# Hybrid decoder trunk: the output of layers 1, 3 and 4 is turned by VectorE and transfers inside SBUF, not by TensorE

## What is computed

```python
for i in range(DEPTH):
    hn = rmsnorm(x, norm_g[i])
    kind, j = i % N_MIXERS, i // N_MIXERS
    if kind == 0:
        y = diff_attention(hn, da_w_in[j], da_w_out[j], ...)
    elif kind == 1:
        y = sliding_window_attention(hn, sw_w_in[j], sw_w_out[j], ...)
    else:
        y = mlstm(hn, ml_w_in[j], ml_b_gates[j], ml_w_out[j], ml_norm_g[j])
    x = x + y
return rmsnorm(x, final_g)

# at the end of a mixer (da; ml has a sigmoid factor more):
o = rmsnorm(o, subln_g) * (1.0 - lambda_init)
o = o.reshape(B, S, WIDTH) * silu(g)
return o @ w_out
```

## Time and profile before

| | |
|---|---|
| median of 3 runs | 1755.09 us (1754.71 to 1756.72) |
| span of the profiled execution | 1753.0 us |
| TensorE busy | 1743.7 us, 99%, 8282 matmuls |
| DVE, ACT, POOL busy | 65%, 52%, 2% |
| transfers | 313 MB, mean 179 GB/s |

### The profile page before, as it was taken

How to read it: one execution, slowest core, us unless ns; L and a number is a source line. 1 busy time by engine, 2 the same in 40 slices (tenths; PEclk the granted TensorE clock), 3 DMA queues, 4 the chain that set the end, 5 groups by cost and what they waited for, 6 DMA issues and landing times.

```text
span 1753.0 us, 25040 instructions
## 1 busy us (share of the span) xinstructions
PE 1743.7 (99%) x8282; PEld 1457.9 (83%) x8282; DVE 1146.3 (65%) x1902; ACT 912.2 (52%) x1424; POOL 40.2 (2%) x99
## 2 busy tenths in 40 slices
PE   9999999999999999999999999999999999999998
PEld 7888888888888888888888888888888888888887
DVE  7766666665558888865655565655666666666655
ACT  7554545454556666645544444454545445454543
POOL 1000000000000000000000000000000000000000
PEclk9999999999999999999999999999999999999999
DMA  8666565655565555457997699866566666656563
GB/s 281 180 179 180 169 183 173 183 167 192 181 185 164 159 156 156 152 180 166 170 164 209 175 166 179 210 172 189 182 188 175 178 178 174 184 169 181 171 212 131
DMA packets 171301, 313.16 MB, mean 179 GB/s; under 512 B 10871, under 2 KB 27837, under 8 KB 171101
## 3 DMA queue, kind: packets, MB, share of 16 engines
q1 hardware_dynamic: 170800, 311.54, 64.5%
q0 software_dynamic: 48, 0.13, 0.2%
q10 hardware_dynamic: 380, 0.56, 0.1%
HBM read 310.10 MB, written 2.10 MB: 178 GB/s over the span
## 4 chain that ended last, share of the span: by engine, by line
PE 99%; DMA 0%; issue 0%; DVE 0%; ACT 0%; SPq 0%; POOLq 0%; POOL 0%; DVEq 0%
PE acc L962 30%; PE acc L964 30%; PE acc L963 30%; PE tp L927 4%; PE sc L963 1%; PE sc L962 1%; PE sc L964 1%; PE sc L994 0%; DMA xres<-in_x_dram 0%; PE sc L1052 0%; PE sc L1050 0%; PE sc L1051 0%; PE sc L1033 0%; PE sc L1032 0%; PE tp L962 0%
## 5 line engine op out<-in xcount | busy, mean ns | idle before, releaser
L1781 DVE TENSOR_TENSOR w_lo<-raw,w_hi 128x1024 fp32r<-128x1024 f32 x583 | 707.8, 1223 | 457.4 <-ACT w_hi L899 456.1
L899 ACT ACTIVATE w_hi<-raw 128x1024 fp32r<-128x1024 f32 x583 | 613.5, 1059 | 451.1 <-PE acc L964 445.0
L962 PE MATMUL acc<-w_hi,xt_hi 128*128 128x512 f32 x1824 | 719.5, 394 | 0.0
L964 PE MATMUL acc<-w_hi,xt_lo 128*128 128x512 f32 x1824 | 711.4, 390 | 0.0
L963 PE MATMUL acc<-w_lo,xt_hi 128*128 128x512 f32 x1824 | 710.3, 389 | 0.0
L964 PEld LDWEIGHTS acc<-w_hi,xt_lo 128*128 128x128 f32 x1824 | 342.3, 188 | 72.6
L963 PEld LDWEIGHTS acc<-w_lo,xt_hi 128*128 128x128 f32 x1824 | 342.8, 188 | 65.8
L962 PEld LDWEIGHTS acc<-w_hi,xt_hi 128*128 128x128 f32 x1824 | 342.6, 188 | 65.6
L962 PE MATMUL acc<-w_hi,ot_hi 128*128 128x512 f32 (+1 forms) x520 | 202.5, 390 | 0.0
L964 PE MATMUL acc<-w_hi,ot_lo 128*128 128x512 f32 (+1 forms) x520 | 200.9, 386 | 0.0
L963 PE MATMUL acc<-w_lo,ot_hi 128*128 128x512 f32 (+1 forms) x520 | 200.7, 386 | 0.0
(11 more groups left out here) (289 smaller groups left out, 1145.6 us busy)
## 6 DMA issues: line engine op xcount, KB each, us to landing
raw<-in_da_w_in_dram SPq DMA_DIRECT2D x255, 512.0 KB, 3.7
raw<-in_ml_w_in_dram SPq DMA_DIRECT2D x96, 512.0 KB, 5.3
raw<-in_sw_w_in_dram SPq DMA_DIRECT2D x72, 512.0 KB, 3.7
raw<-in_da_w_out_dram SPq DMA_DIRECT2D x64, 512.0 KB, 3.7
raw<-in_sw_w_out_dram SPq DMA_DIRECT2D x32, 512.0 KB, 3.6
raw<-in_ml_w_in_dram SPq DMA_DIRECT2D x64, 256.0 KB, 4.8
raw<-in_ml_w_out_dram SPq DMA_DIRECT2D x32, 512.0 KB, 3.8
xres<-in_x_dram SPq DMA_DIRECT2D x3, 512.0 KB, 8.9
```

The costliest lines, as they stand in the source:

```text
L899: act.activation(w_hi[:, q:q + 2, :], raw[:, 2 * p:2 * p + 2, :], ACT.Copy).then_inc(hi_ready, 1)
L962: pe.matmul(out_ap, k_hi, m_hi, start=start, stop=False)
L964: return pe.matmul(out_ap, k_lo, m_hi, start=False, stop=stop)
L1781: dve.tensor_tensor(w_lo[:, two, :], raw[:, two, :], w_hi[:, q:q + 2, :].bitcast(F32), ALU.subtract).then_inc(lo_ready, 1)
```

## The change

After `mix`, DVE turns `gs` by one transpose instruction in 32x32 blocks (`o_turn`) into a free part of `scr` (`o_blocks`): each block is turned where its 32 partitions are, so the blocks still lie in wrong groups of partitions. SP places them: 16 transfers an iteration from `o_blocks` to `th` (`move_o`), each 32 partitions x 2 x 128 elements, four behind each load of slots 10 to 13 of the next iteration or of the output stage (`o_move` = 42). ACT and DVE split from `th` (`o_chunk`) at slot 44, that is 12, and no longer from PSUM at 39. PE's transposes of `gs` in these layers and their PSUM counts go. New semaphores: `o_turned`, `o_moved`, `ot_lo`. ACT's tanh waits for `ot_lo` of the iteration before, since `th` is used twice; PE in the output stage waits for `ot_lo` in place of the PSUM banks. The core of the diff:

```diff
-          g_tanh=35, gate=36, mix=37, o_T=35, o_split=39)
+          g_tanh=35, gate=36, mix=37, o_move=42, o_split=44)
...
-    "tp_0":      ((0, 0, 4), (0, 4, 4), (0, 6, 4), (2, 3, 4)),
-    "tp_1":      ((0, 0, 4), (0, 4, 4), (0, 6, 4), (3, 3, 4)),
+    "tp_0":      ((0, 0, 4), (0, 3, 4), (0, 6, 4), (2, 2, 4)),
+    "tp_1":      ((0, 0, 4), (0, 3, 4), (0, 6, 4), (3, 2, 4)),
...
+        o_blocks = scr_flat[:, 4 * BLK:4 * BLK + T * JW].rearrange("p (t j n) -> p t j n", t=T, j=4)
+        o_moved = th[:].rearrange("p t (j n) -> p t j n", j=4)
+
+        def o_chunk(c):
+            return th[:].rearrange("p t (j k n) -> p (t j) k n", j=4, k=4)[:, :, c, :]
...
+            def move_o(l, i, idx):
+                q = idx + PAIRS * ITER_JOBS[LAYERS[l][0]] - DA["o_move"]
+                if LAYERS[l][0] == "sw" or not 0 <= q < 4:
+                    return
+                if q == 0:
+                    sp.wait_ge(sig["o_turned"], in_iter(l, "o_turned", i, 1))
+                for j in range(4):
+                    sp.dma_start(o_moved[32 * j:32 * j + 32, :, q, :], o_blocks[32 * q:32 * q + 32, :, j, :])\
+                      .then_inc(sig["o_moved"], 16)
...
             def tanh_half(l, J, i, b, dst):
                 act.wait_ge(pairs_done, PAIRS * (J + 1))
+                if LAYERS[l][0] != "sw" and not (isinstance(i, int) and i == 0):
+                    act.wait_ge(sig["ot_lo"], in_iter(l, "ot_lo", i, 0))
...
-            def o_turned_hi(l, i, b, index):
-                turned_hi(lambda c: ot_hi[:, bass.ds(4 * i + c, 1), :].rearrange("p a n -> p (a n)"), b, f"tp_{b}",
-                          index, [scale_col(l, 0), scale_col(l, 1)])
+            def o_turned_hi(l, i):
+                act.wait_ge(sig["o_moved"], in_iter(l, "o_moved", i, 256))
+                for c in range(4):
+                    dst = ot_hi[:, bass.ds(4 * i + c, 1), :].rearrange("p a (j n) -> p (a j) n", n=32)
+                    act.activation(dst, o_chunk(c), ACT.Copy, scale=scale_col(l, c % 2)).then_inc(sig["t_hi"], 1)
...
-                if (i := w.due(DA["o_T"])) is not None:
-                    for b in range(2):
-                        pe.wait_ge(free[f"sc_{b}"], in_iter(l, f"sc_{b}", i, 3))
-                    turn_eight(lambda t: gs[:, t, :], [in_iter(l, f"tp_{b}", i, 3) for b in range(2)])
...
-                        uses = _counts(w.l, name)[1]
-                        pe.wait_ge(free[name], in_iter(w.l, name, ITERS - 2 if p == 0 else ITERS - 1, uses))
+                        pe.wait_ge(sig["ot_lo"], in_iter(w.l, "ot_lo", ITERS - 2 if p == 0 else ITERS - 1,
+                                                         2 if p == 0 else b + 1))
...
+            def o_turn(l, i, uses):
+                for h in range(2):
+                    dve.wait_ge(free[f"sc_{h}"], in_iter(l, f"sc_{h}", i, uses))
+                    if LAYERS[l][0] == "ml":
+                        dve.wait_ge(free[f"tp_{h}"], in_iter(l, f"tp_{h}", i, 2))
+                if not (isinstance(i, int) and i == 0):
+                    dve.wait_ge(sig["o_moved"], in_iter(l, "o_moved", i, 0))
+                op = dve.transpose(o_blocks.rearrange("p t j (k n) -> p t k j n", n=32),
+                                   gs[:].rearrange("p t (k j n) -> p t k j n", k=4, j=4))
+                op.then_inc(sig["o_turned"], 1)
+
+            def o_turned_lo(l, i):
+                dve.wait_ge(sig["o_moved"], in_iter(l, "o_moved", i, 256))
+                for c in range(4):
+                    lo, hi = (buf[:, bass.ds(4 * i + c, 1), :].rearrange("p a (j n) -> p (a j) n", n=32)
+                              for buf in (ot_lo, ot_hi[:].bitcast(F32)))
+                    if c % 2 == 0:
+                        dve.wait_ge(sig["t_hi"], in_iter(l, "t_hi", i, c + 2))
+                    op = dve.scalar_tensor_tensor(lo, o_chunk(c), scale_col(l, c % 2), hi, ALU.mult, ALU.subtract)
+                    if c % 2 == 1:
+                        op.then_inc(sig["ot_lo"], 1)
```

More of the change, by code:

```diff
@@ L92 @@
     "g_scaled":  ((0, 0, 0), (0, 0, 0), (0, 2, 0), (0, 0, 0)),
+    "o_turned":  ((0, 0, 0), (0, 1, 0), (0, 0, 0), (0, 1, 0)),
+    "o_moved":   ((0, 0, 0), (0, 256, 0), (0, 0, 0), (0, 256, 0)),
+    "ot_lo":     ((0, 0, 0), (0, 2, 0), (0, 0, 0), (0, 2, 0)),
     "ot_done":   ((0, 0, 0), (0, 0, 0), (0, 2, 0), (0, 0, 0)),
@@ L470, in load_out @@
                     sp.dma_start(raw[:, 2 * s:2 * s + 2, :], rows_of[:, :, JW * n:JW * n + JW]).then_inc(raw_full[s], 16)
+                    move_o(l, ITERS - 1, q)
                     if l == NL - 1 and q == 2 * PAIRS:
@@ L474, in load_out, with load @@
                                      final_g.rearrange("(a n) -> a n", a=1).to_broadcast([P, D])).then_inc(final_in, 16)
-            def load(w, col, J, pair_of=0):
+            def load(w, col, J, pair_of=0, also=None):
                 for p in range(PAIRS):
@@ L489, in load @@
                           .then_inc(raw_full[s], 16)
+                    if also:
+                        also(p)
             for l, (kind, n) in enumerate(LAYERS):
@@ L497, in iteration @@
                     opening = l == 0 and isinstance(i, int)
+                    moves = None if isinstance(i, int) else lambda p: move_o(l, i - 1, PAIRS + p)
                     if kind == "da":
@@ L502, in iteration @@
                             else:
-                                load(w_in, D * j + JW * i, J + j)
+                                load(w_in, D * j + JW * i, J + j, also=moves if j == 1 else None)
                     elif kind == "sw":
@@ L508, in iteration @@
                         load(w_in, JW // 2 * i, J, pair_of=D // 2)
-                        load(w_in, D + JW * i, J + 1)
+                        load(w_in, D + JW * i, J + 1, also=moves)
                         load(w_in, 2 * D + JW * i, J + 2)
@@ L753, in side_da @@
                 if (i := w.due(DA["o_split"])) is not None:
-                    for b in range(2):
-                        o_turned_hi(l, i, b, in_iter(l, f"tp_{b}", i, 3))
+                    o_turned_hi(l, i)
             def side_sw(w, l):
@@ L869, in side_ml @@
                 if (i := w.due(ML["o_split"])) is not None:
-                    o_turned_hi(l, i, 0, in_iter(l, "tp_0", i, 2))
-                    o_turned_hi(l, i, 1, in_iter(l, "tp_1", i, 2))
+                    o_turned_hi(l, i)
             sides = {"da": side_da, "sw": side_sw, "ml": side_ml}
@@ L1133, in side_ml @@
                         last.then_inc(full[f"tp_{h}"], 1)
[L1134 to L1137, removed]
             sides = {"da": side_da, "sw": side_sw, "ml": side_ml}
@@ L1493, in side_da @@
                     mix(l, i, o_rs)
+                    o_turn(l, i, 3)
                 if (i := w.due(DA["o_split"])) is not None:
-                    for b in range(2):
-                        o_turned_lo(l, i, b, in_iter(l, f"tp_{b}", i, 3), b)
+                    o_turned_lo(l, i)
             def side_sw(w, l):
@@ L1737, in side_ml @@
                     mix(l, i, comb)
+                    o_turn(l, i, 2)
                 if (i := w.due(ML["o_split"])) is not None:
-                    o_turned_lo(l, i, 0, in_iter(l, "tp_0", i, 2), 0)
-                    o_turned_lo(l, i, 1, in_iter(l, "tp_1", i, 2), 1)
+                    o_turned_lo(l, i)
             sides = {"da": side_da, "sw": side_sw, "ml": side_ml}
```

## The result

| | before | changed |
|---|---|---|
| median | 1755.14 us (1754.71 to 1756.72, 4 runs) | 1744.36 us (1744.26 to 1746.05, 4 runs) |
| span of the profiled execution | 1753.0 us | 1744.3 us |

The ratio is 0.9939, with an interval from 0.9927 to 0.9951: 10.8 us less, 0.6%. The profiled execution of the changed kernel is the longest of its four runs (1746.05 us). The spans of the other three are 1742.5 to 1742.6 us. Its trace has the difference in the first microseconds: the sixth product of weights starts at 11.34 us, in the trace of the kernel before at 9.37, and the first ones start some 0.43 us apart in place of 0.23. Why is not shown; the granted clock of these rows is 1.00 in both. One of the four runs of the kernel before (1756.72 us) is longer than its others in the same way, but it has no trace.

The account below looks back on a forecast made before the run. TensorE, busy for 99% of the span, was taken as the bound. Removing 12 blocks x 0.90 us = 10.8 us, with the added work hidden, gave 1755.1 - 10.8 = 1744.3 us; forecast 1742.5 to 1747, range 1742.5 to 1750.

Parts of the forecast that it names:

- What leaves TensorE: Layers 1, 3 and 4 after slot 3: 12 blocks of eight gs transposes, each displacing 0.90 us, 10.8 us off the bound.
- Rivals 3: TensorE's time does not fall: the products have another limit and the gap only moves on, 1755 us; chance 0.04.
- 4: The transposes on TensorE cost by their durations: 2.2 us a block, 26 us, giving 1729 us; chance 0.01.
- The turn: DVE at slot 5, ahead of w_lo: one 128 x 1024 transpose of 1.2 us, twelve times, hidden at no cost.
- rival 2: Slow DVE turn of T us costs 4 x (T - 2.33) in layer 3, 8 x (T - 3.97) elsewhere; chance 0.05.
- The margin at slot 5: Time between w_lo's end on DVE and TensorE's slot 5: 2.33 us left in layer 3 for a 1.2 us turn.
- The issues: SP, slots 10 to 13: 0.37 us each, a load and four moves 1.9 us per 2.72 us slot, lateness worked off.
- The transfer queue of layer 3: Moves add 1.8 to 3 us; landing of loads peaks at 13.4 us against 16.3; ACT waits for loads, TensorE doesn't.
- Rival 1: Layer 3's transfer queue falls too far behind: 1749 us at 7.5 us of moves, 1762 at 12; chance 0.10, half slower.
- The split: At slot 12, reading th in SBUF: operations stay about as long; w_lo keeps 2.2 us of margin in layer 1.

## Why the prediction was right, and where its steps were off

**What leaves TensorE: right.** 12 x 0.90 = 10.8 us was forecast; the medians differ by 10.8, the block put back cost 11.0, and the starts in the trace give 10.9. The forecast of 1744.3 us stands against 1744.36. That they agree to 0.1 us is luck: the four runs lie within 1.8 us, and 0.2 us of late w_lo was not in the sum. Rivals 3 (the gap only moves on) and 4 (a price by durations, 26 us) both fall with these two runs.

**The turn: right.** 1.2 us was taken, between 0.8 and 4.9; it takes 1.246 us. The pauses around it come on top: from the start of mix's last operation to w_lo it was 0.39 us before and is 1.78 now, so w_lo comes 1.39 us later and not 1.2. The run with three turns shows that rival 2 was a real mechanism that lacked only its condition, though its formula is too mild: for 1.25 + 2.56 = 3.8 us it gives 4 x (3.8 - 2.33) = 5.9 us, and 11.5 were measured. It took one cover for all four places of layer 3, and it had no lower clock behind a stall. The page of the Trainium skill that I weighed (VectorE: DVE Perf Modes, "The three transpose paths") has 311 ns for a 128x128 tile in bf16, by which I estimated 2.5 us; the measured 1.246 us for eight such tiles is half of that, so the measurement decides. Its advice to use TensorE for a 128x128 transpose does not hold here: the run that put the block back on TensorE is 11.0 us slower.

**The margin at slot 5: right in kind, mis-sized.** I read it at one place of layer 3 and forecast 2.33 - 1.2 = 1.1 us left. The changed kernel has 0.90, 0.89, 0.06 and 1.07 us left at the four. Its timeline at the second and at the third change of iteration of layer 3, DVE in the one, ACT, DVE and TensorE's weight load in the other:

```profile
1001.93 1.23 DVE L1817 TENSOR_TENSOR w_lo<-raw,w_hi 128x1024 fp32r<-128x1024 f32 x1 [2.73 <-ACT w_hi L925]
...
1009.75 1.25 DVE L1365 STREAM_TRANSPOSE scr<-gs 128x1024 f32<-128x1024 f32 x1
1010.92 4.60 DVE L1817 TENSOR_TENSOR w_lo<-raw,w_hi 128x1024 fp32r<-128x1024 f32 x4
```

```profile
1093.13 1.06 ACT L925 ACTIVATE w_hi<-raw 128x1024 fp32r<-128x1024 f32 x1 [0.76 <-DMA raw<-in_ml_w_in_dram]
1094.22 1.23 DVE L1817 TENSOR_TENSOR w_lo<-raw,w_hi 128x1024 fp32r<-128x1024 f32 x1 [2.56 <-ACT w_hi L925]
...
1102.04 1.25 DVE L1365 STREAM_TRANSPOSE scr<-gs 128x1024 f32<-128x1024 f32 x1
1103.21 2.32 DVE L1817 TENSOR_TENSOR w_lo<-raw,w_hi 128x1024 fp32r<-128x1024 f32 x2
1104.45 0.19 PEld L988 LDWEIGHTS acc<-w_hi,xt_hi 128*128 128x128 f32 x1 [0.29 <-DVE w_lo L1817]
```

At the second, w_lo of slot 5 ends at 1010.92 + 1.22 = 1012.14, 0.9 us before TensorE begins it at 1013.00. At the third it ends at about 1104.4 and TensorE's weight load waited for it, 0.29 us. What differs stands ahead of the side work. ACT waited there for a load, so DVE could begin w_lo of slot 3, the last before the gate, only at 1094.22, 10.23 us before TensorE began slot 5 at 1104.45. At the second it began at 1001.93, 11.07 us before. That takes 0.84 of the 0.90 us.

No row of the kernel before could have shown this: there w_lo of slot 5 ends 3.23 us before TensorE begins it at the second and at the third place alike. The lateness is the change's own. In the run without turn and moves the same w_lo began at 1091.54, 11.07 us before slot 5 at 1102.61, and the loads issued in 1080 to 1086, which landed after 8.9 us (median) in the kernel before, took 11.5 in the changed one. The prediction put the queue's lateness against TensorE's need for raw weights, where 16.3 us were free. It did not put it against DVE's margin, which the turn had already used up but for 0.9 us.

**The issues: mis-sized, and hidden.** I priced a move at the 0.37 us of a load. The row of the changed kernel says otherwise, and so does SP's timeline in layer 3:

```profile
L480 SPq DMA_DIRECT2D th<-scr x192: 585/597/1932, 117.5 to 1670.9; - x192
```

```profile
1013.86 0.38 SPq L509 DMA_DIRECT2D raw<-in_ml_w_in_dram  x1
1014.29 2.52 SPq L480 DMA_DIRECT2D th<-scr  x4
1017.07 0.39 SPq L509 DMA_DIRECT2D raw<-in_ml_w_in_dram  x1
```

A load and four moves take 3.21 us (1013.86 to 1017.07), not 1.9, and a slot of TensorE takes 2.72. So SP does not work its delay off by slot 13, as I wrote; it gains half a microsecond of delay in each of the four slots, on top of the wait for the turn (18.3 us in 12 times by its waits, 1.5 us on average), and catches up later, when it has only loads. It cost nothing by itself because SP runs far ahead: the load of slot 13 went out at 1020.28, 14.5 us before TensorE began that slot at 1034.76 (18.7 us in the kernel before), and it landed after 5.0 us. Rival 1 named the condition, "with issues of over 0.6 us the four slots fall behind". It happened (0.597 us, 0.63 with the step to the next), and four slots were too few to matter. With eight moves they took 5.8 us, and that cost 92 us.

**The transfer queue of layer 3: the right place, at the edge of the range.** Landing after the issue, at its worst (KB each, median us to landing, in the stretch 1042 to 1044, and in 1040 to 1060):

```profile
raw<-in_ml_w_in_dram SPq DMA_DIRECT2D x1, 512.0 KB, 14.4
...
raw<-in_ml_w_in_dram SPq DMA_DIRECT2D x7, 512.0 KB, 13.9
```

Against 10.4 us before, the moves added up to 4.0 us where I took 1.8 to 3.0; the peak of 14.4 lies above the forecast 12 to 13.5 and under the 16.3 that would make TensorE late. In the run without the moves the same stretch has 10.2 us. As forecast, ACT began to wait for loads (31.5 us) and TensorE never waited for one itself; by way of DVE's margin they reached it once, as above. The dear end of rival 1, where a 512-byte packet costs what a 2 KB one does, is refuted: four times as many packets of 128 bytes changed the time by 1.2 us and left the landing in 1040 to 1060 at 13.7 us, against 13.9. The Trainium skill (DMA: Bandwidth & Descriptors, "Why small descriptors are slow (HBM only)") has it that transfers inside SBUF do not suffer from small pieces, and this run agrees. What in the moves, their bytes or their late issue, added the 4 us was not separated.

**The split: right.** Its operations read th in SBUF at 0.497 us on ACT and 0.479 on DVE, against 0.476 on ACT before. By w_lo's ends and TensorE's starts, slot 12 keeps about 2.3 us in layers 1 and 4 (2.2 forecast) and 1.6 to 3.0 in layer 3, where the prediction's rows give 1035.62 - 1031.8 = 3.8. That ACT would wait for moves at all four places of layer 3, 1.5 to 4.0 us, I had not forecast. The mis-sized issues, 1.3 us more in each of four slots, are enough for it, and w_lo's margin at slot 12 took it.

**The two missed expectations** share one cause, the lower clock after a stall. For three turns I had the margins of all four places of layer 3, the 0.06 us of the third too, but no lower clock: 1.7 us. For twice the moves I counted 48 us of waiting and no lower clock. TensorE waited 63 us, and its work took 25.9 us longer; so there the waiting was mis-sized as well, by 15 us.

## What to carry to other kernels

When one engine is full, price a piece of its side work by how far it pushes its neighbours' starts apart, not by its duration: 0.90 us for eight transposes of 0.271 us each. Moving it to engines that run ahead is free up to the smallest margin of any iteration. If the change also delays loads, that margin is not in the trace of before: take the lateness that the change adds off it, on every engine that waits for the loads. Here the small transfers inside SBUF were paid by the issue on their queue, 0.6 us each, and hardly by their pieces: use few and large ones, and compare the sum of their issues with the slot of the full engine. A stall that one does not avoid can cost more than itself, by the lower clock behind it.

## What the runs showed of the hardware

- The issue of a transfer from 32 partitions of SBUF to 32 others takes 0.597 us on SP (median), against 0.373 us for a load of weights (256 KB at line 485, and the same for 512 KB). It was the same for half the bytes (0.597) and about the same for a quarter of the piece length (0.610).
- DVE turns 128 x 1024 f32 in 32x32 blocks in 1.246 us, the rate of its w_lo subtraction (1.225 us for the same shape).
- After a wait of 4.0 us of TensorE (run with twice the moves) and after one of 2.55 us (run with three turns) its granted clock was 0.50 for about 3 us; after one of 1.55 us (same run) it stayed at 1.00. In the run with twice the moves, with a mean granted clock of 0.982, the same matmuls kept TensorE busy 25.9 us longer.
